# Silu of the output gates z: in SBUF after the projection, or in the copy that empties PSUM

## The reference, cut to what matters

```python
for l in range(2):
    h = rms_norm(x, norm_g[l]) * (1 + scale) + shift
    gq, gk, gv, glr, gz, dq, dk, dv, dz = split(h @ w_in[l])
    o_gla  = rms_norm(gla(...), g_out)  * silu(gz)          # [512, 512]
    o_diff = rms_norm(attn(...), g_out) * silu(dz)          # [512, 512]
    x = x + gate * (concat(o_gla, o_diff) @ w_out[l])
```

## Time and profile before

| | us |
|---|---|
| median of 3 runs | 1945.54 (1943.96 to 1948.92) |
| the profiled execution's own time | 1945.24 |
| its span, first to last instruction | 1943.5 |
| PE busy | 1798.3 (93%) |
| DVE busy | 949.8 (49%) |
| POOL busy | 663.2 (34%) |
| ACT busy | 635.0 (33%) |

### The profile page before, as it was taken

One profiled execution on the slowest core, in us unless ns is written; L12 is line 12 of the kernel. 1 busy time (PEld: TensorE's weight loads), 2 busy tenths in 40 slices (PEclk: granted clock), 3 DMA queues, 4 the chain that ended last, 5 costly groups with the idle time before them and its releaser, 6 DMA issues.

```text
span 1943.5 us, 22498 instructions
## 1 busy us (share of the span) xinstructions
PE 1798.3 (93%) x8960; PEld 1500.5 (77%) x8960; DVE 949.8 (49%) x917; ACT 635.0 (33%) x779; POOL 663.2 (34%) x163
## 2 busy tenths in 40 slices
PE   5979987989987789999999899989999989999997
PEld 2868866768976668888888798868888868888886
DVE  4895357565547574545322333674322555454323
ACT  3331344244245333333323322223222243333221
POOL 2231111224221033434344334323434324343342
PEclk9988888989988889999999899999999989999998
DMA  8472111112111022232223232312222312222222
GB/s 319 172 267 82 44 44 44 65 44 87 66 66 44 22 87 87 86 108 86 81 91 109 84 112 86 108 49 103 86 108 86 107 67 87 107 86 94 89 89 73
DMA packets 30914, 180.98 MB, mean 93 GB/s; under 512 B 4466, under 2 KB 4596, under 8 KB 14340
## 3 DMA queue, kind: packets, MB, share of 16 engines
q1 hardware_dynamic: 24480, 161.50, 23.3%
q10 hardware_dynamic: 6372, 18.62, 2.7%
HBM read 178.00 MB, written 2.10 MB: 93 GB/s over the span
## 4 chain that ended last, share of the span: by engine, by line
PE 61%; issue 31%; POOL 4%; DVE 2%; ACT 0%; POOLq 0%; DVEq 0%; ACTq 0%
PE ps L812 20%; PE ps L814 19%; PE ps L813 19%; POOL wl L463 4%; PE ps L843 1%; PE ps L842 1%; PE ps L841 1%; PE ps L918 0%; DVE xl L1250 0%; DVE cv L1650 0%; PE ps L879 0%; DVE y L1287 0%; PE ps L882 0%; PE ps L881 0%; DVE tmp L1659 0%
## 5 line engine op out<-in xcount | busy, mean ns | idle before, releaser
L463 POOL TENSOR_TENSOR wl<-raw,wh 128x2048 fp32r<-128x2048 f32 (+1 forms) x152 | 661.2, 4350 | 1254.3 <-ACT wh L506 1254.2
L812 PE MATMUL ps<-xh,wh 128*128 128x512 f32 x1408 | 559.0, 397 | 41.9 <-DVE xl L1480 15.3
L813 PE MATMUL ps<-xl,wh 128*128 128x512 f32 x1408 | 555.6, 395 | 0.0
L814 PE MATMUL ps<-xh,wl 128*128 128x512 f32 x1408 | 554.5, 394 | 0.0
L506 ACT ACTIVATE wh<-raw 128x2048 fp32r<-128x2048 f32 x152 | 291.2, 1916 | 601.1 <-PE ps L814 530.2
L812 PEld LDWEIGHTS ps<-xh,wh 128*128 128x128 f32 x1408 | 268.9, 191 | 106.9 <-issue 33.5
L814 PEld LDWEIGHTS ps<-xh,wl 128*128 128x128 f32 x1408 | 269.0, 191 | 57.4
L813 PEld LDWEIGHTS ps<-xl,wh 128*128 128x128 f32 x1408 | 269.4, 191 | 55.6
L1614 DVE TENSOR_TENSOR fl<-tmp,fh 128x512 f32 x44 | 194.9, 4430 | 80.9 <-ACT fh L724 80.9
L841 PE MATMUL ps<-wh,xh 128*128 128x256 f32 x608 | 184.3, 303 | 0.0
L842 PE MATMUL ps<-wh,xl 128*128 128x256 f32 x608 | 178.0, 293 | 0.0
(11 more groups left out here) (226 smaller groups left out, 1879.0 us busy)
## 6 DMA issues: line engine op xcount, KB each, us to landing
raw<-ffn_in_stream SPq DMA_DIRECT2D x44, 1024.0 KB, 4.8
raw<-mixer_stream SPq DMA_DIRECT2D x40, 1024.0 KB, 4.8
raw<-layer_stream SPq DMA_DIRECT2D x36, 1024.0 KB, 4.8
raw<-ffn_out_stream SPq DMA_DIRECT2D x32, 704.0 KB, 4.1
ada_late<-w_ada ACTq DMA_DIRECT2D x32, 512.0 KB, 5.2
ada_w<-w_ada SPq DMA_DIRECT2D x8, 1024.0 KB, 18.7
x<-x_t SPq DMA_DIRECT2D x1, 2048.0 KB, 7.8
y_t<-y SPq DMA_DIRECT2D x8, 256.0 KB, 2.2
```

Of the source, the lines that this page charges most:

```text
L463: nc.gpsimd.tensor_tensor(wl[u][:, 0:size], raw[u][:, 0:size], wh[u][:, 0:size].bitcast(F32), ALU.subtract).then_inc(w_ready, 1)
L812: nc.tensor.matmul(bank_ap, w0, x0, start=first, stop=False)
L813: nc.tensor.matmul(bank_ap, w0, x1, start=False, stop=False)
L814: return nc.tensor.matmul(bank_ap, w1, x0, start=False, stop=last)
```

## The change

`empty()` applies Silu to a z tile in the instruction that copies it from PSUM. Stage `z_act` keeps its waits and its signal to DVE and no longer runs an activation.

```diff
@@ empty(stage, j, t), ACT
-                    nc.scalar.activation(dst, bank, ACT.Copy).then_inc(banks_free[u], 1)
+                    nc.scalar.activation(dst, bank, ACT.Silu if stage == "z" else ACT.Copy
+                                         ).then_inc(banks_free[u], 1)
@@ stage "z_act", ACT
                         for u in range(2):
                             act.wait_ge(banks_free[u], emptied(unit0 + PART0["z"] + 2 * g + u, 1))
-                        part = zg[:, :, g * WIDTH:(g + 1) * WIDTH]
-                        nc.scalar.activation(part, part, ACT.Silu).then_inc(z_act, 1)
+                        act.sem_inc(z_act, 1)
```

## The result

The changed kernel takes 1957.6 us (median of 7, 1955.9 to 1962.6), the kernel before 1944.7 us in the same comparison: 1.007 times as long, 95% interval 1.0054 to 1.0086. It is slower, by what was forecast (1956.3). The profiled execution took 1957.57 us, 12.3 us more than that of before, and so did its span.

The account below looks back on a forecast made before the run. TensorE, busy 93% of the span, was taken as the bound; exposed Exp loads of 5.0 us a layer plus 0.5 of clock made 11.0 us, 1945.24 to 1956.3; own range 1952 to 1962, 8-in-10 range 1947 to 1966.

Parts of the forecast that it names:

- Loads and their number: ScalarE in attention: 12 more table loads per layer, 24 for the kernel; busy time up by 23 us.
- Hidden Silu loads, exposed Exp loads: First-half Silu loads run while ScalarE idles before its one wait; Exp loads follow nbias, delaying Exp 1.28 us in odd steps.
- one pair of rows: Trace before: at attention's start a load ran before its instruction's one wait; in step 12 the Exp load began only at nbias.
- The sum of the steps: Attention's delays of PE from exposed loads, added step by step: 5.0 us for a layer, 10.0 for both.
- step 15: Attention: PE already waited 0.96 us for the last combine, so the Exp load costs 1.28 us; stall grows to 2.24.
- step 13: Attention: nbias held up while PE waits 2.60 us, so the Exp load costs 1.28 us; stall behind it about 3.9.
- Step 17 and the layer's end: Last Silu's load delays copy_o(15) by 1.4 us but costs nothing; removed passes at the layer's end covered by 4.85 us.
- step 12: Attention: its Exp load and the Silu ahead go, giving back the preceding step's delay; both together cost -0.1 us.
- The clock: TensorE running at 1.2 GHz instead of 2.4 after longer stalls: 0.5 us for a layer taken, bounds 0 and 3.
- The switch's price: The skill page's 2.66 us per table switch, against the trace's 1283 ns load without drain; would give about 1975 us.
- step 9: Attention: nbias held up by POOL while PE waits 3.54 us; the Exp load counts in full, 1.28 us.
- step 3: Attention: combine has a margin of 0.91 us, so a 1.28 us Exp load delay leaves 0.37 us on PE.

Follow-up runs that it names:

- f_tanh: Changed kernel with Tanh in place of Silu in the z copies, same instructions otherwise; 0.9990 of the kernel before, 1944.3 us.
- e2_loads_alone: Kernel before, both Silu passes kept, plus a one-element Silu ahead of each z copy, written to an existing tile; ratio 1.0072, 1961.5 us.
- b2_early_exp: Changed kernel plus a one-element Exp ahead of the wait for nbias in odd steps, written to an existing tile; 1.0004 of the kernel before, 1946.4 us.
- g_silu_first: Changed kernel with the Silu of a second half ahead of the weights' copy to wh instead of behind it; 1.0045 of the kernel before, 1954.6 us.
- a_no_silu: Kernel before with the two Silu passes over z left out and the copies kept plain; ratio 0.9987, 1942.1 us.
- h_shift: Kernel before with one unused tile allocated ahead of the arena, moving its tiles 32 bytes, no instruction added; ratio 1.0044, 1955.4 us.
- k_max_in_psum: Kernel before with the maximum for nbias written to PSUM instead of SBUF in steps 0 to 11; ratio 0.9970, 1939.8 us.

## Why the prediction was right, point by point

- **Loads and their number.** 24 more loads, 16 on the line of `empty`, 16 on that of `exps`; ScalarE's busy time up by 24.9 us against 23 forecast. Shown by the profile; that they are the whole price, by f_tanh and e2_loads_alone.
- **Hidden Silu loads, exposed Exp loads.** The step rested on one pair of rows. For the Silu loads of first halves the trace after shows it: behind each of them ScalarE still stood idle for 1.21 us or more until PE was through. For the Exp loads it is shown by b2_early_exp, which only changes the side of the wait, and once more by g_silu_first.
- **The sum of the steps.** 5.0 us for a layer forecast, 5.0 and 4.9 measured, no term off by more than 0.21 us; step 15 was the largest miss (1.28 against 1.07). The single stalls were less well forecast than the steps: the one behind step 13 was to be 3.9 us and was 4.42, as PE came to it 0.5 us sooner, and the one at the turn after it fell from 2.10 to 1.11.
- **Step 17 and the layer's end.** The load delayed PE's turn of `o_gla` (3.19 us of wait instead of 1.76) and not the first output product: PE's stall there shrank by 1.4 us instead. The passes removed there were covered, by 5.1 us: shown by a_no_silu, in which the last turn to the first output product took 14.8 us as before. What a_no_silu gained came from the pass around step 12, and the forecast counted that one.
- **The clock** was the loosest term: 0.5 us for a layer. The place was the one named, the stall of step 15; it cost 1.5 us in each layer, of which layer 0 got 1.5 back elsewhere. So the clock came to 0.0 us in one layer and 1.5 in the other; that their sum, 1.5, is near the 1.0 forecast for both is luck. I had judged 2.24 us of stall by one of 2.60 that had not brought the clock down. That reading was too simple; the levels before and after are shown, why the one stall did it and the other did not stays open. Nor does the length of the last stall tell it alone: in layer 1 of g_silu_first a stall of 2.02 us was followed by a part at the full clock.
- **The switch's price.** 2.66 us for a switch, the figure of the Trainium skill's page ScalarE: Activation LUTs, section What ACT_TABLE_LOAD costs, would have given about 1975 by the prediction's estimate (its 14 us for a layer have to be counted from the kernel before: 1945.24 + 28 = 1973). The trace does not agree: its rows show 1.283 us and gaps of 0.01 to 0.02 us around it.

## What to carry to other kernels

ScalarE's busy time does not tell what a table load costs. Ask which side of a wait it falls on: ahead of an activation with one wait it ran during that wait, behind a second wait it ran after it and was paid, in full where PE was already waiting (1.28 us in step 9), less where there was slack behind it (0.42 us in step 3). Moving Silu into the copies turned 3 crossings between table sets in each layer into 15 and cost 0.7%; an activation of a single element ahead of the wait in each odd step took that back. Before putting work on or off an engine, find who sets the stalls of the bound engine: here DVE's queue order, worth 0.9% with not one instruction changed.

## What the runs showed of the hardware

- **A tile 32 bytes further on.** With the arena 32 bytes further on, the kernel took 0.4% longer. Products of the feed-forward stages by group, before and then h_shift (the line numbers are one apart; the products of `fh` with `wl` and of `fl` with `wh`):

```profile
L814 PE MATMUL ps<-fh,wl 128*128 128x512 f32 x352 | 138.0, 392 | 0.0
L813 PE MATMUL ps<-fl,wh 128*128 128x512 f32 x352 | 136.6, 388 | 0.0
```

```profile
L815 PE MATMUL ps<-fh,wl 128*128 128x512 f32 x352 | 140.4, 399 | 0.0
L814 PE MATMUL ps<-fl,wh 128*128 128x512 f32 x352 | 138.7, 394 | 0.0
```

  The products overlap, so what counts is the time from one's start to the next one's: it grew by 2.9 us in all for the first group and by 2.1 for the second, 5.0 of the 8.5 us. `fh` with `wh` got no longer (394 and 392 ns), and those of `xh` with `wh` in the later stages, where `xh` does not lie in the arena, stayed at 391. The same kinds of products in the mixer (`ah`, `bh`, `mh` with `wl`; `al`, `bl`, `ml` with `wh`) took 6 to 7 ns longer each. The mechanism stays open.
- **POOL and DVE.** A [128, 2] product with both operands in SBUF took 4.43 us beside a POOL subtraction, and 0.16 us with one of them in PSUM (k_max_in_psum). The Trainium skill's page SBUF — State Buffer, section SBUF: two separate sides, has it so: VectorE and GpSimd share a port pair that is an exclusive lock, also between a VectorE instruction with two SBUF inputs and a GpSimd one that reads SBUF. The trace agrees: the product ended 0.02 us after POOL's subtraction.
- **Tanh with Exp.** Tanh needed no load beside Exp (f_tanh), Silu did.
